# Two halves of a weight tile woven together: a long and a short matmul alternate one by one in the gate and up products

## What is computed

```python
D_MODEL = 2048
D_FF = -(-(8 * D_MODEL) // (3 * 256)) * 256      # 5632
h2 = rms_norm_2(x, norm2_w[l])
x = x + (jax.nn.silu(h2 @ w_ffn_gate[l]) * (h2 @ w_ffn_up[l])) @ w_ffn_down[l]
```

## Time and profile before

| | |
|---|---|
| median of 3 runs | 2350.07 us (2349.14 to 2352.84) |
| the profiled execution | 2346.51 us |
| its span, from first to last instruction | 2344.7 us |
| TensorE matmul, busy | 2310.0 us (99%) |
| TensorE weight load, busy | 1951.4 us (83%) |
| VectorE, ScalarE busy | 1468.5 us (63%), 1299.5 us (55%) |
| mean granted TensorE clock | 0.996 |
| DMA, mean | 174 GB/s |

### The profile page before, as it was taken

The page is one execution under the profiler, slowest core; times in us unless marked ns, Lnnn a source line. Parts: engine busy times, 40 slices in busy tenths (PEclk is TensorE's granted clock), DMA queues, the critical chain, the costliest instruction groups (busy, mean ns, idle before and its releaser), DMA issues.

```text
span 2344.7 us, 32539 instructions
## 1 busy us (share of the span) xinstructions
PE 2310.0 (99%) x12150; PEld 1951.4 (83%) x12150; DVE 1468.5 (63%) x2547; ACT 1299.5 (55%) x2374; POOL 18.3 (1%) x38
## 2 busy tenths in 40 slices
PE   8999999999999999999999999999999999999998
PEld 8877888788888888877888888888888888888886
DVE  5554565665665666876777666756566566665554
ACT  5644555665655545764556546546555555554444
POOL 1000000000000000000000000000000000000000
PEclk9999999999999999999999999999999999999999
DMA  7555565575445565656453326556666666665554
GB/s 230 171 163 151 171 206 189 153 189 171 127 145 195 154 182 174 188 168 177 141 170 111 107 81 234 198 187 177 191 189 189 189 189 189 189 207 190 192 189 165
DMA packets 239596, 409.07 MB, mean 174 GB/s; under 512 B 21504, under 2 KB 54576, under 8 KB 239056
## 3 DMA queue, kind: packets, MB, share of 16 engines
q1 hardware_dynamic: 235424, 393.07, 55.4%
q0 software_dynamic: 3152, 10.57, 1.2%
q10 hardware_dynamic: 864, 3.35, 0.4%
HBM read 400.65 MB, written 6.29 MB: 174 GB/s over the span
## 4 chain that ended last, share of the span: by engine, by line
PE 94%; DVE 3%; ACT 3%; issue 1%; DMA 0%; ACTq 0%; DVEq 0%
PE banks L390 52%; PE banks L354 17%; PE banks L356 8%; PE banks L384 5%; PE banks L841 1%; PE banks L681 1%; DVE weights_low L325 1%; ACT weights_high L322 1%; PE banks L2343 1%; PE banks L2354 1%; PE banks L1814 1%; PE banks L852 0%; PE banks L1207 0%; PE banks L859 0%; PE banks L861 0%
## 5 line engine op out<-in xcount | busy, mean ns | idle before, releaser
L325 DVE TENSOR_TENSOR weights_low<-weight_ring,weights_high 128x512 fp32r<-128x512 f32 x1464 | 997.4, 691 | 784.9 <-ACT weights_high L322 756.0
L322 ACT CAST weights_high<-weight_ring 128x512 fp32r<-128x512 f32 (+2 forms) x1476 | 904.5, 619 | 954.9 <-PE banks L390 607.5
L390 PE MATMUL banks<-weights_high,hidden_T 128*128 128x512 f32 x2976 | 853.9, 399 | 4.8 <-DVE weights_low L325 2.9
L390 PEld LDWEIGHTS banks<-weights_high,hidden_T 128*128 128x128 f32 x2976 | 550.3, 188 | 126.1 <-issue 9.9
L354 PE MATMUL banks<-hidden_T,weights_high 128*128 128x512 f32 x1728 | 543.3, 396 | 1.3 <-DVE weights_low L325 0.8
L390 PE MATMUL banks<-weights_low,hidden_T 128*128 128x512 f32 x1488 | 461.6, 391 | 0.0
L356 PEld LDWEIGHTS banks<-hidden_T,weights_low 128*128 128x128 f32 x1728 | 324.6, 188 | 76.7
L356 PE MATMUL banks<-hidden_T,weights_low 128*128 128x256 f32 x1728 | 339.5, 278 | 0.0
L390 PEld LDWEIGHTS banks<-weights_low,hidden_T 128*128 128x128 f32 x1488 | 280.1, 188 | 60.8
L354 PEld LDWEIGHTS banks<-hidden_T,weights_high 128*128 128x128 f32 x1728 | 263.1, 189 | 2.3 <-DVE weights_low L325 1.4
L390 PE MATMUL banks<-weights_high,ffn_high 128*128 128x512 f32 x344 | 106.3, 390 | 1.6 <-DVE weights_low L325 1.6
(11 more groups left out here) (426 smaller groups left out, 1801.3 us busy)
## 6 DMA issues: line engine op xcount, KB each, us to landing
weight_ring<-in_w_in SPq DMA_DIRECT2D x168, 512.0 KB, 3.6
weight_ring<-in_w_gla_in SPq DMA_DIRECT2D x96, 512.0 KB, 3.8
weight_ring<-in_w_gate SPq DMA_DIRECT2D x88, 512.0 KB, 3.6
weight_ring<-in_w_ffn_up SPq DMA_DIRECT2D x88, 512.0 KB, 3.7
weight_ring<-in_w_down SPq DMA_DIRECT2D x88, 512.0 KB, 3.8
weight_ring<-in_w_mla_in SPq DMA_DIRECT2D x48, 512.0 KB, 3.7
weight_ring<-in_w_gla_out SPq DMA_DIRECT2D x32, 512.0 KB, 4.5
weight_ring<-in_w_mla_out SPq DMA_DIRECT2D x32, 512.0 KB, 4.3
```

The costliest lines, as they stand in the source:

```text
L322: nc.scalar.copy(hi, raw).then_inc(high_ready, 1)
L325: nc.vector.tensor_tensor(lo, raw, hi.bitcast(F32), ALU.subtract).then_inc(low_ready, 1)
L390: last = pe.matmul(ps[:, b + t, 0:width], a[:, t * P:(t + 1) * P], w, start=(k == 0 and n_th == 0), stop=(k == kt - 1 and n_th == 2))
```

## The change

All but a few tiles of the `HALVES_APART` chunks get another order of the same eight matmuls. Long ones and short ones alternate, and a short one never goes to the block of its neighbour: long 0, short 1, long 2, short 3, long 1, short 0, long 3, short 2. The number of matmuls, their shapes and what they add to are the same. The first tile of each chunk (k == 0) keeps the old order, and so do the three tiles that run ahead.

```diff
+            def multiply_alternating(self, pe, n, k):
+
+                if k == 0:
+                    self.multiply_apart(pe, n, k, (0, 1))
+                    return self.multiply_apart(pe, n, k, (2, 3))
+                _, kt, _, _, width, acts, _ = self.chunks[n]
+                _, q = self.place_of(n, k)
+                pe.wait_ge(low_ready, q + 1)
+                hi, lo = w_high[:, q % PARTS, :], w_low[:, q % PARTS, :]
+                ahi, both = acts(k)
+                final = k == kt - 1
+                out = [ps[:, bank, :] for bank in self.banks(n)]
+                for f, g in ((0, 1), (2, 3), (1, 0), (3, 2)):
+                    pe.matmul(out[f], hi[:, f * P:(f + 1) * P], both, start=False, stop=False, skip_group_check=True)
+                    last = pe.matmul(out[g][:, 0:S], lo[:, g * P:(g + 1) * P], ahi, start=False, stop=final, skip_group_check=True)
+                return last
+
             def multiply(self, pe, i, n, k, b):
...
                 if turned == HALVES_APART:
-                    for fs in ((0, 1), (2, 3)):
-                        last = self.multiply_apart(pe, n, k, fs)
+                    last = self.multiply_alternating(pe, n, k)
```

## The result

The changed kernel takes 2356.3 us (median; 2354.51 to 2359.61), the kernel before 2349.87 us in the same rounds: 1.0028 times as long, 95% interval 1.0020 to 1.0036. It is 6.4 us slower. The profiled execution has a span of 2353.9 us.

A forecast was written before the change was run, and what follows sets the result against it. TensorE was taken to bound the kernel. Switches at +2.2 us and the wait at 0 to -2.0 were taken as 0 in the middle, leaving a median of 2350 us, range 2340 to 2357.

The forecast's parts named there:

- the case of 0.20: Slower outcome, chance 0.20: alternating tiles cost more at each switch of kind, 2357 us, up to 2366.6.
- What bounds the kernel: TensorE, busy 99% of the span, never idle in gate and up; a small gain or loss per tile reaches the end.
- the one on neighbours: Alternating tiles: only a matmul's cost beside the other kind could change the time; no kind differed by more than 0.01 us.
- 1.35 ns for each switch: Change between long and short in a tile: eight switches instead of four, 5.4 ns more per tile, +2.2 us.
- The wait: Counter check in the middle of a tile, 403 of them gone: 0 to -2.0 us.
- The rival that every switch costs: Alternating tiles: each matmul differs from the one before in operand, buffer and bank range; +7 us, 2357 us, chance 0.20.
- Its sign in the profile: Window of 100 us in gate and up: some 571 matmuls if switches cost 1.5 ns per matmul; 574 to 578 if unchanged.
- The cover of long for short: Alternating tiles: long matmuls' slack covers short ones' loads; 20.2 ns less per tile, -8.1 us, 2342 us, chance 0.23.
- the case of 2304: Alternating tiles: loads run two matmuls ahead, at most 114 ns less per tile, -46 us, chance 0.05.
- the sentence at the end: Prediction's caveat: wrong if matmul costs depend on more than the next neighbour, say a bank written a while before; no size.

The follow-up runs named there:

- e1: Changed kernel with the first tile of each chunk alternating too, only the three tiles that run ahead in the old order: 2347.35 us, 0.9991 of the kernel before.
- e4: TensorE alone, no other engine at work, twenty stretches of up to 16 tiles: old order 1393.3 ns a tile, alternating order 1386.7 or 1413.3.
- e3: Changed kernel with each short matmul right behind the long one of the same block, so neighbours write the same bank: 2357.43 us, 1.0035.
- e9: TensorE alone, seven other orders of four long and four short, each begun four ways: one pace each, 1396.7 to 1413.3 ns; alternating order 1386.7 or 1413.3.
- e6: Kernel of e1 with the old order in one more tile, the first of the sixth chunk of gate and up: 2354.59 us, 1.0021.

## Why the prediction was wrong

It said 2350, no change that counts; it is 2356.3, slower by 0.28%. The time lies inside the range of 2340 to 2357, and the case of 0.20 came true.

*What bounds the kernel* was right: TensorE, with nothing late, so that each nanosecond of a tile came through. What a tile lost came through in full: by their starts the alternating tiles lost 6.3 us, and the kernel lost 6.4.

*The step that failed* is the one on neighbours: "All that could change the time to first order is thus whether a matmul costs another time beside a neighbour of the other kind." The trace of before does hold all four kinds of neighbours, and they do cost alike; the conclusion does not follow. With the same neighbours in e1 and in the changed kernel, a tile costs 1386.7 or 1413.3, by what ran some time ahead. The step built on it, 1.35 ns for each switch and so 5.4 more with eight, took a property of the whole order (1393.3 against the bare 1386.7, 6.7 more) for a price per switch. At the fast pace the eight switches cost nothing. The numbers there were also off. The 1393.8 is 1393.3 by the exact starts, an effect of rows of 0.01 us. The 228.4 for a long one is 226.7: the row of 40.20 us begins with the first matmul's whole duration,

```profile
2159.90 0.50 PE banks L390
```

and the other 175 share 39.70 us. With 226.7 and the 118.7 of the short ones, which is right for that stage, the same step would have given 1381.6 for four of each, 11.8 ns for four switches, and so +4.7 us, 2355. That would have been nearer by luck, by a price per switch that does not exist.

*The wait* was put at 0 to -2.0 us. It is worth nothing: the old order costs 1393.3 per tile with TensorE alone, where no tile checks a counter (e4), and the same in the kernel with two checks. The 0.12 against 0.11 us on which the -2.0 stood is a part of the order's own pattern.

*The rival that every switch costs* had the size nearly right, +7 us, and the cause wrong. Its sign in the profile came up, 568 matmuls in a window where I had put 571; but e1 has more switches and is 9 us faster than the changed kernel. *The cover of long for short* gave no gain either: the best pace is the bare sum of the two kinds' own costs with TensorE alone, and no order went below it. The short ones did get cheaper, 116.7 ns in e1 against 120.0, but the long ones took 230.0 against 226.7 and paid it back. At the slow pace of the changed kernel the short ones take the same 116.7 and the long ones 236.7, so the 6.7 ns a pair between the two paces are all in the long ones. No load of the alternating tiles ran further ahead, so the case of 2304 has nothing for it. The Trainium skill's gap of N / 2.4 + 2.5 ns, given there for a single matmul ("TensorE: Matmul & The Clock Gate", "Back-to-back issue gap") is below the measurement with TensorE alone as well, 215.8 against 226.7 and 109.2 against 120.0; both are 13.3 ns over the columns at 2.4 GHz. So those 13 ns are no effect of other engines in this kernel.

*What the sentence at the end warned of*, a cost that depends on more than the next neighbour, was the truth, though not through the distance between two writes of a bank, which e3 changed without effect. It was named and given no price.

Why the pace has two values stays open. All seven paces of a tile in e4 and e9 are multiples of 3.33 ns (8 periods of 2.4 GHz) to the accuracy of the starts, which looks like two processes falling into step, but no run shows what they are. Nor is it known what sets the pace behind a pause.

## What to carry to other kernels

In a stretch that is bound by TensorE, measure the time per tile from starts, for each order and each chunk: a mean over the stage hides two paces. One odd tile can set the pace for hundreds of microseconds behind it, so a change of order is to be measured with the odd tiles that it leaves, and an order with one pace (here the old one, 0.5% above the bare sum) is the safer choice over one with two. The best version found, alternating in nearly every tile (e1), came out at 0.9991 of the kernel before, at the edge of what can be told from no change.

## What the hardware showed unexpectedly

- The same loop of matmuls runs at 1386.7 or 1413.3 ns per tile on TensorE alone, behind the same pause (e9); there is nothing between.
- It stays at its pace for as long as nothing else comes between: some 20 us alone, and in e1 and e6 through the gate and up chunks. What an inserted tile does to the pace follows from its order and from its place in a rhythm of three pairs (57 old tiles, no exception).
- Four long and four short matmuls cost between 1386.7 and 1413.3 ns by their order alone, at a granted clock of 1.00 throughout, with no relation to the number of switches.
- With TensorE alone a pure stretch costs N / 2.4 + 13.3 ns per matmul, at 512 columns and at 256 alike (226.7 and 120.0 ns, e4). The long ones of L390 in the kernel before cost the same 226.7; the short ones of L384 cost 118.7, less than alone, and why is open.
